# Output projection split further, stores on another queue, earlier first segments and first expert weights, in a two-block transformer kernel

## The chip, the cores and the metric

One core of one Trainium2 chip runs the whole program as one launch. The metric is the device time of a launch in microseconds (us); lower is better. The kernel before takes 3806.11 us, the median of three runs (3799.67 to 3806.13).

## The reference

1024 tokens of width 1024 in fp32 pass through two blocks.

- First block, two layers. `x = x + gate_a * (mixed @ w_out)`, where `mixed` (1024 wide) holds gated linear attention in its first 512 columns and softmax attention of 4 heads (causal, 128-query blocks) in the last 512; then a squared-ReLU MLP of width 4096. Shifts, scales and gates come from `silu(c) @ w_ada`.
- Second block, one layer. `z = rms_norm(h) @ w_in` feeds three mixers: a spatial gating unit (384 wide), a gated linear recurrence (384) and a state-space model with a GELU and a sigmoid gate (256). Each is normalised and `h = h + concat(...) @ w_out_2`. Then a router picks one of 4 groups and 2 of its 4 experts for each token (16 experts, each `(silu(x @ w_gate) * (x @ w_up)) @ w_down` of width 512), and a final norm.

## The kernel before, in words

Every engine has its own hand-written program; steps wait for each other by named semaphores (`S_.out_pe.at("turn", l, t, half)` is "TensorE has done this turn"). Tokens go in 8 tiles (`NT`) of 128, widths in 8 chunks (`KC`) of 128. A product of two fp32 operands takes either one whole fp32 matmul per chunk (two instruction records in the trace) or, split, three matmuls in the rounded type float32r: high x high, high x low, low x high (`split_mm`).

**Attention** (`sp_attention`, L1225 to L1254; `act_att_out`, L1383) has 32 steps, 4 heads of 8 query tiles in the order 7, 0, 6, 1, 5, 2, 4, 3. ScalarE writes each 128x128 result into one of two buffers, SyncE stores it to the scratch array `mixed` (64 KB), and ScalarE takes a buffer again only when its store of two steps ago has landed. All transfers of SyncE are on one queue. In between SyncE issues the loads of `w_ada` pieces (1 MB each, 16 in layer 0 and 4 in layer 1), the next head's queries, `w_out` (at steps 10 and 13, 2 MB each) and `x` (16 and 19, 2 MB each). `before_output` has SyncE, and the ScalarE step that rounds `w_out`, wait until the last two stores have landed.

**Output projection** (`pe_output`, `pe_residual`, L1473) goes tile by tile: turn 8 blocks of `mixed` (`pe_turn_mixed`), 8 chunks of matmul into two banks (the two halves of the width), turn the previous tile's normed rows. Tile 0 is whole fp32; in tiles 1 to 7 chunks 4 to 7 are whole and come first in each half, chunks 0 to 3 are split. The high part of `w_out` lies in the rows that tiles 6 and 7 of the next stage's input take later (`high_place`), the low part overwrites `w_out` itself (`dve_out_low`). VectorE does, per tile, two gated additions for each half (L1570, L1572), the low part of the turned `mixed` (`dve_mixed_low`, L1587), and the norm. The ring of `mixed` has one place: its next load is issued when the turn is done.

**End of the mixers in block two.** VectorE: gating product, scaling of `w_out_2` chunks 3 to 6, the four sums of the state-space output (L2787), two products of 3072 elements (`dve_driven`, L2478 and L2480), three scans, the last product and the last two chunks of `yT` (`dve_ssm_done`). ScalarE scales the other chunks of `w_out_2` (`act_route_weights`, L2873) after all four sigmoids. `before_route` makes every engine wait for all of it; then `pe_route` starts: per tile the norms, 16 whole matmuls in 6 segments (half 0 and half 1, each with chunks 0 to 2, 3 to 5, 6 and 7), turns and router logits.

**Experts.** 24 steps (`STEPS`), each with two blocks of 64 rows (sides 0 and 1) and each side with its own expert's weights, 2 MB each for gate, up and down, in two halves. The expert of a block is known only after the placement (`dve_placement`), so GpSimd loads weights and rows with indirect transfers; an index out of bounds skips the load when the block has the same expert as the one before. In the first step nothing is skipped. GpSimd's order is: rows of step 0, gate, up, rows of step 1, down, gate of step 1.

Of the kernel before, what the change touches and what calls it, by code (L numbers as in the profile page):

```python
# [1406 lines left out]
def output_views(k):  # L1407
# [9 lines left out]
    V.mT_hi, V.mT_lo = (k.rounded(shaped(k.weights[:, 3, n:n + SPLIT * P], (SPLIT, P))) for n in (0, KC * P))  # L1417
# [29 lines left out]

def pe_turn_mixed(k, l, t):
    S_, E, V = k.S, k.pe, k.outs
    E.wait_ge(S_.mixed_in.at(l, t))  # L1450
    for half in range(2):
        if t > 0:
            E.wait_ge(S_.out_act.at("mT", l, t - 1, half))
        if t > 1 and half == 0:
            E.wait_ge(S_.out_dve.at("mT", l, t - 1))
# [3 lines left out]
def pe_first_residual(k, l):  # L1459
# [5 lines left out]
    i.then_inc(*S_.out_pe.up("whole", l))  # L1465
# [43 lines left out]
def act_mixed_turned(k, l, t):  # L1509
    S_, E, V = k.S, k.act, k.outs  # L1510
    for half in range(2):
# [3 lines left out]
        place = V.mT_hi if half == 0 and t > 0 else V.mT[:, 4 * half:4 * half + 4, :]  # L1515
        k.nc.scalar.activation(flat(place), k.ps[half], ACT.Copy).then_inc(*S_.out_act.up("mT", l, t, half))  # L1516
# [2163 lines left out]
```

## Time and profile before

| | |
|---|---|
| Median of three runs | 3806.11 us |
| The profiled execution | 3802.61 us, of which the span is 3801.3 us |
| TensorE busy | 3602.4 us, 95% of the span |
| VectorE, ScalarE, GpSimd busy | 47%, 27%, 18% |
| Chain that ended last | TensorE 82%, VectorE 7%, DMA 4%, ScalarE 2%, GpSimd 2% |

The span is the profiled part of one execution on the chip. The chain is followed back from the last instruction, at each step to what released it. In the timeline a number in brackets is the engine's idle time before the instruction and what ended it.

### The profile page before, as it was taken

The numbers are of one execution on the slowest core, as the hardware profiler recorded it, in microseconds if no ns is written. First come the engines' busy times: TensorE is split into PE (matmuls) and PEld (weight loads), VectorE is DVE, ScalarE is ACT, GpSimd is POOL, SyncE is SP. The second block draws the span as 40 slices with busy tenths as digits, with TensorE's granted clock in tenths as the row PEclk, the third lists the DMA queues.
The fourth block names the chain that finished last, engine by engine and source line by source line (L and its number), as shares of the span: only waits on it lengthen the run. The fifth ranks groups of instructions, "written<-read, shape, count | busy, mean of one in ns | idle before, by whom it ended". The sixth has DMA issues, their size and how long they took to land.

```text
span 3801.3 us, 42410 instructions
## 1 busy us (share of the span) xinstructions
PE 3602.4 (95%) x17043; PEld 2377.4 (63%) x17043; DVE 1780.8 (47%) x3353; ACT 1035.7 (27%) x1872; POOL 693.1 (18%) x688
## 2 busy tenths in 40 slices
PE   5999899999999999998999999999999896999994
PEld 4666556777778776665567888888764553333331
DVE  5666764455555546666444334444446632000003
ACT  2444223322222224443323222222230411111111
POOL 1122001111111102211011111111010002555555
PEclk9999899999999999999999999999999997999997
DMA  6000550222222240002411111111400304887524
GB/s 218 30 29 28 181 193 28 69 79 83 78 80 90 70 163 26 26 20 87 165 34 45 45 45 56 45 45 45 136 3 0 101 28 168 319 301 259 201 82 149
DMA packets 226788, 365.55 MB, mean 96 GB/s; under 512 B 54712, under 2 KB 156946, under 8 KB 214304
## 3 DMA queue, kind: packets, MB, share of 16 engines
q1 hardware_dynamic: 176080, 240.20, 18.9%
q0 software_dynamic: 47232, 121.75, 9.0%
q8 instruction: 134, 2.20, 0.2%
q10 hardware_dynamic: 3280, 0.89, 0.1%
q14 instruction: 62, 0.51, 0.0%
HBM read 519.99 MB, written 44.04 MB: 148 GB/s over the span
## 4 chain that ended last, share of the span: by engine, by line
PE 82%; DVE 7%; DMA 4%; ACT 2%; POOL 2%; issue 2%; SPq 1%; DVEq 0%; POOLq 0%; ACTq 0%
PE psum L225 63%; PE psum L3354 13%; PE psum L233 4%; DVE arena L475 3%; DMA arena<-in_w_ada 2%; DMA tmp_mixed<-arena 1%; DVE arena L1042 0%; POOL stat L268 0%; DVE arena L416 0%; POOL stat L270 0%; POOL arena L3487 0%; PE psum L2769 0%; DMA arena<-tmp_hn,row_i 0%; DMA arena<-in_x 0%; SPq L392 0%
## 5 line engine op out<-in xcount | busy, mean ns | idle before, releaser
L225 PE MATMUL psum<-arena_r,arena_r 128*128 128x512 f32 x4096 | 1298.5, 397 | 1.0 <-POOL weight_ring_r L1838 1.0
L225 PEld LDWEIGHTS psum<-arena_r,arena_r 128*128 128x128 f32 x4096 | 768.2, 188 | 188.3 <-issue 1.9
L225 PE MATMUL psum<-arena 128*128 128x128 f32 (+9 forms) x4020 | 827.5, 382 | 11.3 <-DVE arena L1121 3.8
L225 PEld LDWEIGHTS psum<-arena 128*128 128x128 f32 (+1 forms) x4020 | 506.8, 193 | 288.7 <-issue 193.8
L225 PE MATMUL psum<-arena_r,weight_ring_r 128*128 128x512 f32 x1360 | 492.5, 399 | 0.0
L1881 DVE TENSOR_TENSOR arena<-arena,psum 128x512 f32<-128x512 f32 x512 | 335.2, 683 | 171.2 <-PE psum L225 171.1
L225 PE MATMUL psum<-weight_ring_r,arena_r 128*128 128x512 f32 x1024 | 408.7, 399 | 0.0
L1838 POOL TENSOR_TENSOR weight_ring_r<-weight_ring,arena_r 128x1024 fp32r<-128x1024 f32 x64 | 154.9, 2422 | 1126.9 <-ACT arena_r L1788 1126.9
L3354 PE MATMUL psum<-arena 128*64 128x512 f32 x1536 | 341.5, 597 | 6.4 <-DMA arena<-in_expert_w_gate,be_i 5.6
L1872 DVE TENSOR_TENSOR arena_r<-arena,arena_r 128x512 fp32r<-128x512 f32 x128 | 88.6, 692 | 462.7 <-ACT arena_r L1826 462.7
L225 PEld LDWEIGHTS psum<-arena_r,weight_ring_r 128*128 128x128 f32 x1360 | 255.7, 188 | 71.8 <-issue 13.4
L233 PEld LDWEIGHTS psum<-const,arena 128*128 128x128 f32 (+1 forms) x1439 | 171.8, 155 | 152.3 <-issue 87.3
L225 PE MATMUL psum<-weight_ring,arena 128*128 128x128 f32 (+2 forms) x1024 | 262.9, 408 | 2.5 <-DVE arena L1164 1.6
L268 POOL TENSOR_SCALAR stat<-stat 128x1 f32<-128x1 f32 (+1 forms) x120 | 43.9, 366 | 1196.6 <-ACT arena L1531 457.1
L233 PE MATMUL psum<-const,arena 128*128 128x128 f32 (+1 forms) x1439 | 214.3, 290 | 46.4 <-ACT arena L1374 16.0
L225 PE MATMUL psum<-arena,weight_ring 128*128 128x512 f32 x544 | 243.4, 600 | 7.1 <-ACT weight_ring L1516 7.1
L1802 ACT ACTIVATE arena_r<-weight_ring 128x2048 fp32r<-128x2048 f32 x32 | 61.4, 1917 | 680.5 <-DVE weight_ring L1853 680.5
L3354 PEld LDWEIGHTS psum<-arena 128*64 128x64 f32 x1536 | 108.9, 138 | 216.4 <-issue 212.7
L3445 DVE TENSOR_TENSOR arena<-arena,psum 128x512 f32<-128x512 f32 x24 | 16.5, 689 | 446.7 <-issue 287.1
L225 PEld LDWEIGHTS psum<-weight_ring_r,arena_r 128*128 128x128 f32 x1024 | 192.3, 188 | 41.8
L225 PEld LDWEIGHTS psum<-weight_ring,arena 128*128 128x128 f32 x1024 | 150.6, 197 | 85.6 <-issue 85.6
L225 PEld LDWEIGHTS psum<-arena,weight_ring 128*128 128x128 f32 x544 | 102.4, 192 | 125.1 <-issue 114.4
(380 smaller groups left out, 3372.7 us busy)
## 6 DMA issues: line engine op xcount, KB each, us to landing
weight_ring<-in_w_mlp_up SPq DMA_DIRECT2D x32, 1024.0 KB, 5.9
weight_ring<-in_w_mlp_down SPq DMA_DIRECT2D x32, 1024.0 KB, 5.0
arena<-in_w_ada SPq DMA_DIRECT2D x24, 1024.0 KB, 7.3
arena<-in_w_ada SPq DMA_DIRECT2D x40, 512.0 KB
arena<-in_w_in SPq DMA_DIRECT2D x6, 2048.0 KB, 18.6
tmp_ys<-arena SPq DMA_DIRECT2D x24, 512.0 KB
arena<-in_w_out SPq DMA_DIRECT2D x4, 2048.0 KB, 9.5
arena<-tmp_mixed SPq DMA_DIRECT2D x16, 512.0 KB, 3.3
```

Of the source, the lines that this page charges most:

```text
L225: i = self.nc.tensor.matmul(out, lhs, rhs, start=start and n == 0, stop=stop and n == len(pairs) - 1)
L233: i = self.nc.tensor.transpose(out, in_, self.ident(in_.shape[0]))
L268: k.nc.gpsimd.tensor_scalar(out, total, 1.0 / width, EPS, ALU.mult, ALU.add).then_inc(*G.up())
L475: ins = k.nc.vector.scalar_tensor_tensor(acc, V.w[:, c, :], k.cond[:, c:c + 1], acc if c else V.bias, ALU.mult, ALU.add)
L1802: k.nc.scalar.activation(down_high(k, n), V.down_w[down_slot(n)], ACT.Copy).then_inc(*S_.ff_act.up("down_hi", l, n))
L1838: k.nc.gpsimd.tensor_tensor(V.up_lo[up_slot(n)][here], w[here], V.up_hi[here].bitcast(F32), ALU.subtract).then_inc(*S_.ff_pool.up("up_lo", ...
L1872: v.tensor_tensor(V.u_lo[b][:, blk, cols], V.u[b][:, blk, cols], V.u_hi[b][:, blk, cols].bitcast(F32), ALU.subtract).then_inc(*out.up("u_l ...
L1881: v.tensor_tensor(xs, xs, ff_bank(k, down_use(m) + j), ALU.add).then_inc(*out.up("down", l, m, t, half))
L3354: i = k.nc.tensor.matmul(bank[at(c, BLOCK), :], left[:, b, at(c, BLOCK)], w[c][:, b, at(a, 512)], start=b == 0, stop=b == n - 1)
L3445: v.tensor_tensor(V.su, V.sg[s % 2], k.ps[2], ALU.mult).then_inc(*S_.ex_dve.up("su", s))
```

## The change

Six edits: (1) the attention's stores go from SyncE to GpSimd's queue; (2) in the output projection chunks 4 to 7 are split as well in tiles 2 to 5, their high part in the rows of tiles 4 and 5, and their half of `w_out` (2 MB) is loaded again for tiles 6 and 7; tiles 2 to 7 begin with split chunks 0 to 3, tile 1 has both whole halves first; (3) the first of `dve_driven`'s two products moves ahead of the state-space sums; (4) ScalarE scales chunks 0 to 2 between the sigmoids, and TensorE does the first segments of both halves of tile 0 before it waits for the rest; (5) SyncE loads expert 0's weights of side 0 ahead (gate during the route, up and down at its end), gate and down change places in memory, and GpSimd's first step takes side 1 first and skips side 0 where the first block is expert 0's; (6) the rows of step 1 are gathered before the up weights.

```diff
         E.wait_ge(S_.att_act.at("out", l, n))
-        nc.sync.dma_start(d["mixed"][at(qt), 512 + h * MV:512 + (h + 1) * MV], V.out[b]).then_inc(*(S_.att_out0 if b == 0 else S_.att_out1).dma(l, n))
...
 def pool_attention(k, l):
     before_attention(k, k.pool, l)
     pool_ada_zero(k, k.ada_att[l], l)
+    for n in range(ATT):
+        h, qt, _ = att_step(n)
+        b = n % 2
+        k.pool.wait_ge(k.S.att_act.at("out", l, n))
+        k.nc.gpsimd.dma_start(k.d["mixed"][at(qt), 512 + h * MV:512 + (h + 1) * MV], k.att.out[b]).then_inc(*(k.S.att_out0 if b == 0 else k.S.att_out1).dma(l, n))
...
-    return (V.h_lo if c < 2 else V.h_hi)[:, at(c % 2, 4), (NT - 2) * P:]
+    first = (NT - 2 if c < SPLIT else NT - 4) * P
+    return (V.h_lo if c % 4 < 2 else V.h_hi)[:, at(c % 2, 4), first:first + 2 * P]
...
+def all_split(t):
+
+    return 2 <= t < NT - 2
...
+        if t == NT - 2:
+            E.wait_ge(S_.out_pe.at("out", l, NT - 3, 1))
+            nc.sync.dma_start(V.w[:, SPLIT:], d["w_out"][l].rearrange("(k p) n -> p k n", p=P)[:, SPLIT:]).then_inc(*S_.w_again.dma(l))
...
+def pe_out_split(k, l, t, half, chunks, start):
+    S_, E, V = k.S, k.pe, k.outs
+    if start:
+        E.wait_ge(S_.out_dve.at("gated", l, t - 1, half))
+    E.wait_ge(S_.out_dve.at("w_lo", l, chunks[-1]), S_.out_dve.at("mT", l, t, chunks[-1] // 4))
+    parts = at(half, 2)
+    return k.split_mm(by_parts(k.ps[2 + half]), [(V.mT_hi[:, c, :], V.mT_lo[:, c, :], high_place(k, c)[:, parts], by_parts(V.w_lo[:, c, :])[:, parts])
+                                                 for c in chunks], start=start, stop=not start)
...
 def pe_residual(k, l, t):
     S_, E, V = k.S, k.pe, k.outs
     E.wait_ge(S_.out_act.at("mT", l, t, 1))
-    for half in range(2):
-        E.wait_ge(S_.out_dve.at("gated", l, t - 1, half))
-        k.mm(k.ps[2 + half], [(V.mT[:, c, :], V.w[:, c, at(half, 512)]) for c in range(SPLIT, KC)], stop=False)
-        E.wait_ge(S_.out_dve.at("w_lo", l), S_.out_dve.at("mT", l, t))
-        parts = at(half, 2)
-        i = k.split_mm(by_parts(k.ps[2 + half]), [(V.mT_hi[:, c, :], V.mT_lo[:, c, :], high_place(k, c)[:, parts], by_parts(V.w_lo[:, c, :])[:, parts])
-                                                  for c in range(SPLIT)], start=False)
-        i.then_inc(*S_.out_pe.up("out", l, t, half))
+    first, rest = range(SPLIT), range(SPLIT, KC)
+    if all_split(t):
+        for half in range(2):
+            pe_out_split(k, l, t, half, first, True)
+            pe_out_split(k, l, t, half, rest, False).then_inc(*S_.out_pe.up("out", l, t, half))
+    elif t == 1:
+        for half in range(2):
+            i = pe_out_whole(k, l, t, half, True)
+        i.then_inc(*S_.out_pe.up("whole", l, 1))
+        for half in range(2):
+            pe_out_split(k, l, t, half, first, False).then_inc(*S_.out_pe.up("out", l, t, half))
+    else:
+        for half in range(2):
+            pe_out_split(k, l, t, half, first, True)
+        for half in range(2):
+            pe_out_whole(k, l, t, half, False).then_inc(*S_.out_pe.up("out", l, t, half))
...
-    for c in range(SPLIT):
+    for c in range(KC):
         k.nc.scalar.activation(high_place(k, c), by_parts(V.w[:, c, :]), ACT.Copy).then_inc(*S_.out_act.up("w_hi", l, c))
...
+def dve_out_low(k, l, part):
     S_, E, V = k.S, k.dve, k.outs
-    E.wait_ge(S_.out_pe.at("whole", l))
-    for c in range(SPLIT):
+    E.wait_ge(S_.out_pe.at("whole", l, part))
+    for c in range(part * SPLIT, (part + 1) * SPLIT):
         E.wait_ge(S_.out_act.at("w_hi", l, c))
-        i = k.nc.vector.tensor_tensor(by_parts(V.w_lo[:, c, :]), by_parts(V.w[:, c, :]), high_place(k, c).bitcast(F32), ALU.subtract)
-    i.then_inc(*S_.out_dve.up("w_lo", l))
+        k.nc.vector.tensor_tensor(by_parts(V.w_lo[:, c, :]), by_parts(V.w[:, c, :]), high_place(k, c).bitcast(F32), ALU.subtract).then_inc(*S_.out_dve.up("w_lo", l, c))
...
+    for half in range(2 if all_split(t) else 1):
+        here = slice(4 * half, 4 * half + 4)
+        E.wait_ge(S_.out_act.at("mT", l, t, half))
+        k.nc.vector.tensor_tensor(flat(V.mT_lo[:, here]), k.ps[half], flat(V.mT_hi[:, here]).bitcast(F32), ALU.subtract).then_inc(*S_.out_dve.up("mT", l, t, half))
...
     for t in range(NT - 2):
+        if t == 0:
+            dve_out_low(k, l, 1)
         dve_residual(k, l, t + 1)
...
+def dve_driven_half(k):
+    S_, E, V = k.S, k.dve, k.rec
+    E.wait_ge(S_.rec_act.at("h"), S_.rec_dve.at("ix"))
+    k.nc.vector.tensor_tensor(V.i, V.i, V.h, ALU.mult).then_inc(*S_.rec_dve.up("half driven"))
+
...
 def dve_driven(k):
     S_, E, V = k.S, k.dve, k.rec
-    v = k.nc.vector
-    E.wait_ge(S_.rec_act.at("h"), S_.rec_dve.at("ix"))
-    v.tensor_tensor(V.i, V.i, V.h, ALU.mult).then_inc(*E.up())
-    E.wait_ge(S_.rec_act.at("th"), E.last)
-    v.tensor_tensor(V.i, V.i, V.th, ALU.mult).then_inc(*S_.rec_dve.up("driven"))
+    E.wait_ge(S_.rec_act.at("th"), S_.rec_dve.at("half driven"))
+    k.nc.vector.tensor_tensor(V.i, V.i, V.th, ALU.mult).then_inc(*S_.rec_dve.up("driven"))
...
         for half in range(2):
             E.wait_ge(S_.ssm_pe.at("glu", c, half))
             k.nc.scalar.activation(flat(V.gs[:, c, 4 * half:4 * half + 4]), k.ps[2 * c + half], ACT.Sigmoid, bias=k.cols[:, 50 + c:51 + c]).then_inc(*S_.ssm_act.up("glu", c, half))
+        act_route_weights(k, (S_.w_out_b, S_.w_out_c)[c], ((0, 1, 2), (7,))[c])
...
+def segment(t, j):
+
+    return ((0, 0), (1, 0), (0, 1), (0, 2), (1, 1), (1, 2))[j] if t == 0 else (j // 3, j % 3)
...
 def sp_route(k):
     nc, S_, E, V = k.nc, k.S, k.sp, k.rt
+    before_route(k, E)
     for t in range(NT):
+        if t == 1:
+            sp_first_expert(k, "gate")
         E.wait_ge(S_.rt_dve.at("hn", t))
         nc.sync.dma_start(k.d["hn"][at(t), :], V.hn).then_inc(*S_.hn_out.dma(t))
+    E.wait_ge(S_.rt_pe.at("seg", 6 * NT - 1))
+    sp_first_expert(k, "up")
+    sp_first_expert(k, "down")
...
 def pe_rt_residual(k, t):
     S_, E, V = k.S, k.pe, k.rt
     for j in range(6):
-        half, (lo, hi), u = j // 3, SEGMENTS[j % 3], 6 * t + j
+        half, part = segment(t, j)
+        (lo, hi), u = SEGMENTS[part], 6 * t + j
         if u >= 4:
             E.wait_ge(S_.rt_dve.at("seg", u - 4))
-        E.wait_ge(S_.rt_dve.at("w"), S_.rt_act.at("w", 2 if hi < KC else 7))
+        if u < 4:
+            E.wait_ge(S_.ssm_act.at("glu", u // 2, u % 2))
+        if part == 0:
+            E.wait_ge(S_.rt_act.at("w", 2))
+        else:
+            if u == 2:
+                pe_rt_norms(k, 0)
+            E.wait_ge(S_.rt_dve.at("w"), S_.ssm_dve.at("done"), S_.rec_dve.at("y"))
+        if part == 2:
+            E.wait_ge(S_.rt_act.at("w", 7))
         k.mm(k.ps[u % 4], [(k.yT[:, c, at(t)], V.w[c][:, at(half, 512)]) for c in range(lo, hi)]).then_inc(*S_.rt_pe.up("seg", u))
...
-    v.memset(V.same[:, 0:1], 0.0)
+    v.tensor_scalar(V.same[:, 0:1], V.be[:, 0:1], 0.0, None, ALU.is_equal)
...
-    V.w = {"gate": [k.arena[:, c * n:(c + 1) * n] for c in range(2)], "up": [ring[:, c * n:(c + 1) * n] for c in range(2)],
-           "down": [k.arena[:, (2 + c) * n:(3 + c) * n] for c in range(2)]}
+    V.w = {"gate": [k.arena[:, (2 + c) * n:(3 + c) * n] for c in range(2)], "up": [ring[:, c * n:(c + 1) * n] for c in range(2)],
+           "down": [k.arena[:, c * n:(c + 1) * n] for c in range(2)]}
...
+def sp_first_expert(k, what):
+    k.nc.sync.dma_start(k.ex.w[what][0], k.d[f"expert_w_{what}_2"][0][0].rearrange("(p k) n -> p (k n)", p=P)).then_inc(*first_arrived(k, what).dma())
...
+def sides(s):
+
+    return (1, 0) if s == 0 else (0, 1)
...
     if s > 0:
         E.wait_ge(S_.ex_pe.at(what, s - 1, h))
+    else:
+        E.wait_ge(first_arrived(k, what).at())
     rows = k.d[f"expert_w_{what}_2"][0].rearrange("e (p h k) n -> (e p h) (k n)", p=P, h=2)
     n = KC * D_EXP // 2
-    for c in range(2):
+    for c in sides(s):
         b = c * STEPS + s
         nc.gpsimd.indirect_dma_start(out=V.w[what][c][:, at(h, n)], out_offset=None, in_=rows, in_offset=bass.IndirectOffsetOnAxis(ap=k.place.be_i[:, h, b:b + 1], axis=0),
...
     E.wait_ge(S_.place_dve.at("be"))
     pool_load(k, "gate", 0, 0)
     pool_load(k, "gate", 0, 1)
+    pool_gather(k, 1)
     pool_load(k, "up", 0, 0)
     pool_load(k, "up", 0, 1)
-    pool_gather(k, 1)
     pool_load(k, "down", 0, 0)
...
-    E.wait_ge(arrived(k, what, h).at(s, 1))
+    E.wait_ge(arrived(k, what, h).at(s, sides(s)[1]))
...
-    act_route_weights(k)
...
     dve_route_weights(k)
+    dve_driven_half(k)
     dve_ssm_out(k)
...
```

## Rows read from the trace of the kernel before

**Rows 1.** The chain of waits, layer 0's attention: start, duration, what.
```profile
448.13 3.45 PE psum L225 x15
...
497.64 9.52 DMA tmp_mixed<-arena
```

**Rows 2.** The windows view: stretch, length, busy time of each engine, clock, DMA share, GB/s.
```profile
478.58:511.71 33.13, 31.37 (x173) 20.83 (x173) 26.29 (x60) 10.36 (x28) 0.00 (x0) 0.96 0.93 327
1829.38:1858.28 28.90, 28.16 (x159) 17.89 (x158) 14.19 (x41) 10.31 (x28) 0.00 (x0) 1.00 0.58 196
```

**Rows 3.** The timeline of ScalarE, then TensorE, where a store's landing is waited for.
```profile
507.24 0.37 ACT L1383 ACTIVATE arena<-psum,stat 128x128 f32<-128x128 f32 x1 [5.12 <-DMA tmp_mixed<-arena]
...
507.66 1.05 PE L225 MATMUL psum<-const,arena 128*128 128x1 f32 x8 [1.76 <-ACT arena L1383]
```

**Rows 4.** Groups of VectorE in layer 1's attention (1774 to 1886), by form.
```profile
L1356 DVE COPY arena<-psum 128x512 f32<-128x512 f32 x19 | 12.9, 677 | 2.3 <-PE psum L233 2.3
```

**Rows 5.** The chain of waits, layer 0's output projection.
```profile
543.99 14.02 PE psum L225 x32
...
604.83 12.59 PE psum L225 x40
617.42 1.75 PE psum L233 x16
...
661.29 5.59 PE psum L225 x24
```

**Rows 6.** The timeline of VectorE in the output projection.
```profile
551.21 4.63 DVE L1580 TENSOR_TENSOR arena_r<-arena,arena_r 128x1024 fp32r<-128x1024 f32 x4 [10.83 <-PE psum L225]
...
603.12 0.69 DVE L1570 TENSOR_TENSOR arena<-psum,gate 128x512 f32<-128x512 f32 x1 [4.80 <-PE psum L225]
...
604.46 0.68 DVE L1587 TENSOR_TENSOR weight_ring_r<-psum,weight_ring_r 128x512 fp32r<-128x512 f32 x1
```

**Rows 7.** DMA issues, 2955 to 2966: size, microseconds to landing.
```profile
weight_ring<-in_w_out SPq DMA_DIRECT2D x1, 2048.0 KB, 7.9
```

**Rows 8.** The chain of waits, end of layer 1's attention.
```profile
1883.54 3.77 DMA arena<-tmp_mixed
1889.72 16.45 PE psum L225 x32
```

**Rows 9.** The timeline of all engines before and in the route.
```profile
2982.60 2.77 ACT L2448 ACTIVATE arena<-arena 128x3072 f32<-128x3072 f32 x1
...
2987.46 0.75 DVE L2787 SCALAR_TENSOR_TENSOR arena<-arena,small,psum 128x512 f32<-128x512 f32 x1 [4.42 <-PE psum L2777]
...
2993.37 3.35 DVE L2478 TENSOR_TENSOR arena<-arena 128x3072 f32<-128x3072 f32 x1
...
3002.35 4.25 ACT L2873 ACTIVATE weight_ring<-weight_ring,small 128x1024 f32<-128x1024 f32 x4
...
3014.98 2.27 PE L225 MATMUL psum<-const,arena 128*128 128x1 f32 x10 [13.25 <-ACT arena L2946]
...
3032.88 1.17 PE L225 MATMUL psum<-const,arena 128*128 128x1 f32 x10
```

**Rows 10.** The timeline of all engines at the experts' first step.
```profile
3188.21 0.99 POOL L3306 DMA_INDIRECT arena<-in_expert_w_gate,be_i  x1 [0.30 <-issue]
...
3191.33 0.60 ACT L3405 ACTIVATE arena<-psum 128x512 f32<-128x512 f32 x1 [0.26 <-PE psum L233]
...
3196.90 9.59 PE L3354 MATMUL psum<-arena 128*64 128x512 f32 x32 [5.60 <-DMA arena<-in_expert_w_gate,be_i]
```

**Rows 11.** The chain of waits there.
```profile
3197.29 15.67 DMA arena<-tmp_hn,row_i
...
3214.97 12.48 PE psum L3354 x48
...
3228.13 10.45 PE psum L3354 x48
```

**Rows 12.** DMA queues, 3184 to 3232: packets, MB, share of 16 engines.
```profile
q0 software_dynamic: 3383, 14.74, 78.8%
```

More of the change, by code:

```diff
@@ L1233, in sp_attention @@
     for n in range(ATT):
-        h, qt, _ = att_step(n)
-        b = n % 2
+        h = n // NT
         if n % 2 == 1 and n // 2 + 4 < 2 * len(place.pieces):
@@ L1416, in output_views @@
     V.w_lo = k.rounded(V.w)
-    V.mT_hi, V.mT_lo = (k.rounded(shaped(k.weights[:, 3, n:n + SPLIT * P], (SPLIT, P))) for n in (0, KC * P))
+    V.mT_hi, V.mT_lo = (k.rounded(shaped(k.weights[:, 3, n:n + KC * P], (KC, P))) for n in (0, KC * P))
 SPLIT = 4
@@ L1454, in pe_turn_mixed @@
         if t > 1 and half == 0:
-            E.wait_ge(S_.out_dve.at("mT", l, t - 1))
+            E.wait_ge(S_.out_dve.at("mT", l, t - 1, 0))
+        if all_split(t - 1) and half == 1:
+            E.wait_ge(S_.out_dve.at("mT", l, t - 1, 1))
         k.turn4(k.ps[half], V.mixed, half).then_inc(*S_.out_pe.up("turn", l, t, half))
@@ L1464, in pe_first_residual @@
         i = k.mm(k.ps[2 + half], [(V.mT[:, c, :], V.w[:, c, at(half, 512)]) for c in range(SPLIT)], stop=False)
-    i.then_inc(*S_.out_pe.up("whole", l))
+    i.then_inc(*S_.out_pe.up("whole", l, 0))
     for half in range(2):
@@ L1468, in pe_first_residual, with pe_out_whole @@
         i.then_inc(*S_.out_pe.up("out", l, 0, half))
+def pe_out_whole(k, l, t, half, start):
+    S_, E, V = k.S, k.pe, k.outs
+    if start:
+        E.wait_ge(S_.out_dve.at("gated", l, t - 1, half))
+    elif t == NT - 2:
+        E.wait_ge(S_.w_again.at(l))
+    return k.mm(k.ps[2 + half], [(V.mT[:, c, :], V.w[:, c, at(half, 512)]) for c in range(SPLIT, KC)], start=start, stop=not start)
+def pe_out_split(k, l, t, half, chunks, start):
+    S_, E, V = k.S, k.pe, k.outs
+    if start:
+        E.wait_ge(S_.out_dve.at("gated", l, t - 1, half))
+    E.wait_ge(S_.out_dve.at("w_lo", l, chunks[-1]), S_.out_dve.at("mT", l, t, chunks[-1] // 4))
+    parts = at(half, 2)
+    return k.split_mm(by_parts(k.ps[2 + half]), [(V.mT_hi[:, c, :], V.mT_lo[:, c, :], high_place(k, c)[:, parts], by_parts(V.w_lo[:, c, :])[:, parts])
+                                                 for c in chunks], start=start, stop=not start)
 def pe_residual(k, l, t):
@@ L1514, in act_mixed_turned @@
             E.wait_ge(S_.out_pe.at("out", l, t - 1, 1))
-        place = V.mT_hi if half == 0 and t > 0 else V.mT[:, 4 * half:4 * half + 4, :]
-        k.nc.scalar.activation(flat(place), k.ps[half], ACT.Copy).then_inc(*S_.out_act.up("mT", l, t, half))
+        place = V.mT_hi if half == 0 and t > 0 or all_split(t) else V.mT
+        k.nc.scalar.activation(flat(place[:, 4 * half:4 * half + 4, :]), k.ps[half], ACT.Copy).then_inc(*S_.out_act.up("mT", l, t, half))
 def act_out_high(k, l):
@@ L1618, in dve_output @@
     k.dve.wait_ge(k.S.x_all_in.at(l, 4))
-    dve_out_low(k, l)
+    dve_out_low(k, l, 0)
     dve_residual(k, l, 0)
@@ L2921, in pe_route @@
     S_, E, V = k.S, k.pe, k.rt
-    before_route(k, E)
-    pe_rt_norms(k, 0)
     pe_rt_residual(k, 0)
@@ L3024, in dve_rt_residual @@
     for j in range(6):
-        half, seg, u = j // 3, j % 3, 6 * t + j
+        (half, seg), u = segment(t, j), 6 * t + j
         xs, bank = V.x[:, t, at(half, 512)], k.ps[u % 4]
@@ L3294, in pool_gather, with first_arrived @@
                                  in_offset=bass.IndirectOffsetOnAxis(ap=k.place.row_i[:, s:s + 1], axis=0)).then_inc(*rows_arrived(k, s).dma(s))
+def first_arrived(k, what):
+    return {"gate": k.S.eg_first, "up": k.S.eu_first, "down": k.S.ed_first}[what]
+def sp_first_expert(k, what):
+    k.nc.sync.dma_start(k.ex.w[what][0], k.d[f"expert_w_{what}_2"][0][0].rearrange("(p k) n -> p (k n)", p=P)).then_inc(*first_arrived(k, what).dma())
+def sides(s):
+    return (1, 0) if s == 0 else (0, 1)
 def pool_load(k, what, s, h):
```

12 lines of the change are left out of this document (4 added, 8 removed).

## The prediction

> **What bounds the kernel now.** I read the page first: TensorE is busy in nearly every one of the 40 slices, and the chain that ended last is mostly TensorE. So time goes in two ways only: fewer or cheaper matmuls where TensorE never waits, or less of the few gaps in which it does. The chain cut to stretches shows which is which. In the output projection it is TensorE alone, 12.59 us of matmuls and 1.75 us of turns for each tile [rows 5]: a full engine, with gaps only around tiles 0 and 1. In layer 0's attention a small store takes 9.52 us and the chain runs through it [rows 1, 3]. Before the route the chain is VectorE's, and TensorE stood 13.25 us idle [rows 9]. At the experts' start it is transfers: TensorE waits 5.60 us for gate weights, and then the second gather needs 15.67 us to land [rows 10, 11]. The 24 expert steps after that are TensorE's and are untouched.
>
> **Edit 1, stores on GpSimd's queue.** What holds the store in layer 0 is the queue that it shares with loads of 1 and 2 MB: the head from 478.58 takes 33.13 us at a DMA share of 0.93, the same head in layer 1, with 4 `w_ada` loads instead of 16, takes 28.90 us [rows 2]. Not all of the 4.23 us is the store: the head before it (448.13 to 478.58, 30.45 us [rows 1, 2]) has VectorE's `w_ada` sums too and no such wait. I take 33.13 - 30.45 = 2.7 us, with 0 and 4.2 as ends. In GpSimd's queue are 32 issues for each layer; the trace has no plain GpSimd transfer. The nearest row is an indirect one, 0.99 us to issue [rows 10], against a lap of 28.90 / 4 = 7.2 us for two stores, and GpSimd is idle there [rows 2]. The last store lands perhaps 1 to 2 us later, which delays ScalarE's rounding of `w_out` and SyncE's loads; tile 0's 14.02 us of whole matmuls [rows 5] hide that. SyncE keeps its waits for `out`, so its loads come no sooner. One cost could speak against the edit: a GpSimd transfer that is held up by VectorE. VectorE's copies in attention take 677 ns for 512 elements [rows 4], 1.3 ns an element, read from PSUM. The Trainium skill, "SBUF — State Buffer", section "SBUF: two separate sides", says that VectorE's two-port modes, as in fp32 copies from SBUF to SBUF, lock GpSimd out so that it can't write descriptors. By that rule copies at this rate from PSUM shouldn't lock it, so the sum stays; were it otherwise it would be the third rival.
>
> **Edit 2, chunks 4 to 7 split.** A split chunk is three matmuls. 24 of them take 5.59 us [rows 5], 0.233 each; a tile with all chunks split has 48, 11.18 us, against 12.59 us: 1.41 us less. Four tiles: 5.64 us for each layer. Three things take from it.
> First, VectorE's low part of `mixed` was needed only after the whole chunks; now tiles 2 to 7 begin with split ones. VectorE ends it at 604.46 + 0.68 = 605.14, and TensorE began that tile at 604.83 [rows 5, 6]. With the semaphore that is 0.4 us of stall in each of tiles 3 to 7, 2.0 us. In the all-split tiles VectorE has another 0.68 us, but the second half's part is wanted 2.8 us later: hidden.
> Second, tile 2: VectorE's second `dve_out_low` (4.63 us [rows 6]) can start only when tile 1's whole chunks are done, 5.59 us before that tile's end; then come the four additions, 0.69 us each, and the low part. It ends about -5.6 + 0.15 + 4.6 + 2.7 + 0.7 = 2.6 us after the tile, and TensorE wants it 1.75 us after: 0.8 us. ScalarE's four more roundings fall before it is next needed.
> Third, the reload. 2 MB landed in 7.9 us with little beside it [rows 7]. TensorE wants it after turns, stall and 24 matmuls: 1.75 + 0.4 + 5.59 = 7.7 us after tile 5's end, at which it is issued: 0.3 us. The next `mixed` tile queues behind it on SyncE's queue and is wanted 6.8 us of whole matmuls later: hidden.
> Together 5.64 - 2.0 - 0.8 - 0.3 = 2.5 us for each layer, 5.1 us for both. Ends: +11.3 if no stall shows, -4.8 if each of six tiles stalls by 1.0 us and the reload by 2.
>
> **Edits 3 and 4, the hand-over to the route.** `h` is ready at 2982.60 + 2.77 = 2985.37, and VectorE stands 4.42 us idle before 2987.46 [rows 9]. The first product (3.35 us) fits from 2985.4 to 2988.8; the first sum is 1.3 us late, the last one at 2992.7 isn't. So the whole chain after it is 3.35 us shorter, and the norms start at about 3011.6 instead of 3014.98. SyncE's load of `x` waits on the same chain and moves with it.
> The two first segments are 6 of tile 0's 16 whole matmuls, 16 of which take 14.02 us [rows 5]: 5.26 us. ScalarE's scaling of three chunks is done by 3005.5 even if it starts no sooner than now (3002.35, 1.06 us each [rows 9]), and TensorE has the segments done by 3010.8, inside its gap. What is left is the 17.9 us from 3014.98 to 3032.88 [rows 9] less 5.26 us: tile 0 ends at 3011.6 + 12.6 = 3024.2, 8.6 us sooner. In this the slow clock stays as it is: norms took 2.27 us where the next ones took 1.17, and layer 1's 16 whole matmuls after a wait of 3.77 us took 16.45 us instead of 14.02 [rows 5, 8]. The gap that remains is about 1 to 4 us; if the clock stays high the gain is 11.0 us, if the product's move is lost elsewhere 5.3. The later tiles run as before. The 2 MB of gate weights on SyncE's queue go between two `hn` stores that 16 whole matmuls, 14 us, keep apart; at 7.9 us they are hidden.
>
> **Edits 5 and 6, the first expert step.** Now the chain is gate (3196.90), second gather (lands 3212.96), up weights' matmuls from 3214.97 [rows 10, 11]. 14.74 MB move on GpSimd's queue in 48 us, nearly all in the first 32 [rows 12]; of them 6 MB are side 0 of step 0 and are skipped if the first block is expert 0's. The gate's first half is then 1 MB instead of 2 and issued one place sooner, before 3188.21 [rows 10]: it lands before or near 3192.5, when the turned rows are ready too (3191.33 + 0.60 = 3191.93). Gate: 3192.5 + 9.59 = 3202.1. The second gather, now ahead of 4 issues and behind 2 MB, has landed by then. Its turns take 1.0, so the up matmuls start at 3203.1, 11.9 us sooner. They took 12.48 us for 48 where the steady 48 take 10.45 [rows 11]: with no gap ahead of them up to 2.0 us more come back. The rest of the loads comes at the same spacing as before while TensorE is 12 us ahead, so some of this may be lost again: I take 12.5 us, ends 7.5 (gate no sooner, the gather alone) and 14. The preloads of up and down, 4 MB, have the placement's 20 us to land. The new `tensor_scalar` instead of a memset is some 0.1 us.
>
> **Sum.** 2.7 + 5.1 + 8.6 + 12.5 = 28.9 us. The profiled execution took 3802.61 us around a span of 3801.3, so it would take 3773.7. The median of the runs is 3.5 us above it: 3806.11 - 28.9 = **3777 us**.
>
> **Rivals.**
> The start of the experts gives less: the first block isn't expert 0's and nothing is skipped, so the preload does nothing (the change doesn't do what it says), or the loads behind bind. Only the gather's place counts, 7.5 us: 3782. For it: 2 MB of gate took until 3196.9. Against: 128 assignments for each expert on average, so an empty expert 0 is unlikely.
> The output projection costs instead of giving: at the bound of -4.8 us the total is 19 us, 3787. For it: VectorE and TensorE hand over at each tile's end. Against: only 0.4 us is seen missing.
> The other side: stores from GpSimd are slow. ScalarE was ready for its buffer at 502.1, 4.5 us after the store's issue at 497.64, and TensorE lost 1.76 us of a landing of 9.52 [rows 1, 3]; so a landing up to some 7.8 us costs nothing. If each pair's store took 9.52 us, 16 pairs in 2 layers would lose 1.76 each, 56 us in place of the gain: 3806 + 56 - 26 = 3836. It decides from a landing of 7.8 us, and turns the whole slower from 8.6 (26 / 32 above it). Against: 64 KB alone, on a queue of its own, with 0.99 us of issue.
>
> **How the numbers follow.** The sum as worked out 0.72, less at the experts 0.12, output at a loss 0.10, slow stores 0.04, something unseen 0.02. Adding the ends, the gain lies between 8 and 40.5 us; both ends need every term at its worst or best, so I cut to 3764 to 3791. A measurement of this kernel tells 0.2%, 7.6 us, from nothing: faster 0.93, within 0.2% 0.03, slower 0.04.
>
> **What would show each step.** After: (1) no wait of ScalarE's L1383 for a store, layer 0's third head near 30.4 us, stores landing in under 4.5 us; (2) 11.2 us for tiles 2 to 5 of both layers, a gap of 0.3 to 0.5 before each tile from 2 on, nearly 1 before tile 2, and before tile 6's whole chunks under 1; (3, 4) the norms of tile 0 near 3.4 us sooner than the rest of the program's shift, six matmuls ahead of them, tile 0 done 8 to 11 us sooner; (5, 6) gate weights no longer the wait, gathers landing in about 5 us, the first up matmuls 12 to 14 us sooner after placement. Wrong would be: a tile period that stays at 14.3, a clock that drops at the new gaps, an expert step 1 that waits for its gate weights, or a store of 8 us.

## The result, and the profile after

The changed kernel takes 3775.69 us, the median of four runs (3775.22 to 3780.64), against 3806.12 us for the one before in the same session (3799.67 to 3808.91): a ratio of 0.9925 [0.9908, 0.9943], 0.75% less. Forecast were 3777 us. Its profiled execution took 3776.03 us, 26.6 us less than that of the kernel before. Numbers in steps below are from the two profiled executions; at each joint I subtract the start of the same piece of work after from its start before, so the growth of this offset from joint to joint is what a stretch gave. "The logits" stands for the start of the router's last logit matmuls (x16, 3.6 us).

The head of the page: the span, then each engine's busy time, share and instructions.

```profile
span 3774.7 us, 42602 instructions
...
PE 3589.2 (95%) x17107; PEld 2385.5 (63%) x17107; DVE 1794.1 (48%) x3369; ACT 1042.6 (28%) x1880; POOL 729.1 (19%) x752
```

TensorE is 13 us less busy, so half of the gain is time in which it used to stand.

| Stretch | Forecast gain, us | Measured |
|---|---|---|
| Layer 0's attention (edit 1) | 2.7 | 3.7 |
| Output projection, layers 0 and 1 (edit 2) | 2.5 and 2.5 | -0.66 and -0.53 |
| To the end of the scans (edit 3) | 3.35 | 3.46 |
| The row above and on to tile 2 of the route (edits 3, 4) | 8.6 | 9.87 |
| Placement to step 1 (edits 5, 6) | 12.5 | 12.46 |
| All else | 0 | 1.72 |
| Sum (the 3.46 us are in the 9.87), span | 28.9 | 26.6 |

"All else" is small pieces of both signs (start-up +1.2, MLPs -1.7, layer 1's attention and tile 0 +1.9, the rest of the route +1.7, the tail -1.4); I take no cause for them from one execution each.

**Attention.** The chain of waits in layer 0 (start, duration, what) answers to [rows 1]: the store is gone from it.

```profile
477.39 3.45 PE psum L225 x15
...
507.85 3.45 PE psum L225 x15
```

The windows view (stretch, length, busy time of PE, PEld, DVE, ACT, POOL, clock, DMA share, GB/s) answers to [rows 2] with its first line (the second is for the output projection below):

```profile
477.39:507.85 30.46, 29.95 (x175) 19.69 (x174) 25.80 (x59) 10.24 (x28) 4.32 (x8) 1.00 0.93 342
556.79:565.64 8.85, 8.85 (x17) 3.92 (x18) 0.85 (x2) 0.00 (x0) 0.00 (x0) 0.81 0.03 11
```

The third head takes 30.46 us where it took 33.13, at the same DMA share of 0.93. The waits view of ScalarE between 412 and 545 us had its L1383 wait four times, 10.8 us in all, for a store's landing; after, one wait of 1.1 us is left, that of the rounding before the output projection. All 64 stores of attention, in the view of their line (issue time minimum, median, maximum in ns; then the landings):

```profile
L1262 POOL DMA_DIRECT2D tmp_mixed<-arena x64: 540/540/807, 421.9 to 1881.8; - x64
...
DMA to landing us min/median/max: 1.9/3.5/6.2
```

**Output projection.** The chain of layer 0 answers to [rows 5], with its last two lines from layer 1:

```profile
539.07 14.02 PE psum L225 x32
556.79 8.85 PE psum L225 x16
...
573.69 11.44 PE psum L225 x48
587.32 11.45 PE psum L225 x48
...
614.59 11.45 PE psum L225 x48
626.05 8.03 DMA arena<-in_w_out
634.12 7.15 PE psum L225 x16
643.46 12.71 PE psum L225 x40
657.04 5.59 PE psum L225 x24
...
1886.08 15.64 PE psum L225 x32
1905.43 8.85 PE psum L225 x16
```

An all-split tile has 48 matmuls in 11.44 us and a period of 13.63 (573.69 to 587.32), where a tile had 12.59 and 14.34. Tiles 6 and 7 take 13.05 (634.12 + 7.15 - 628.22, the timeline's start of tile 6) and 12.71 us. But tile 1 lost: its 16 whole records, now all in front, take 8.85 us at a mean granted clock of 0.81 (second line of the windows above), where the same 16 take 7.15 us in tile 6.

**Before the route.** The timeline (start, duration, instruction, in brackets the idle time before it and what ended that) answers to [rows 9]:

```profile
2989.43 3.35 DVE L2529 TENSOR_TENSOR arena<-arena 128x3072 f32<-128x3072 f32 x1
...
3000.04 5.39 PE L225 MATMUL psum<-weight_ring,arena 128*128 128x512 f32 x12 [0.55 <-ACT weight_ring L2922]
3007.61 1.25 PE L225 MATMUL psum<-const,arena 128*128 128x1 f32 x10 [2.18 <-ACT arena L3014]
3008.71 10.53 PE L225 MATMUL psum<-weight_ring,arena 128*128 128x512 f32 x20
...
3019.08 1.17 PE L225 MATMUL psum<-const,arena 128*128 128x1 f32 x10
```

One product is left after the sums; six matmuls (12 records) stand in the old gap; ahead of the norms 2.18 us of idleness are left of 13.25, and the norms take 1.25 us where they took 2.27. The 20 records behind them are slow: 10.53 us, where the later tiles' 32 take 13.98, which is 8.74 for 20. The windows view of TensorE's clock shows why:

```profile
3009.00:3012.37 3.37, 3.37 (x5) 1.34 (x4) 1.41 (x4) 0.63 (x1) 0.70 (x1) 0.50 0.64 21
```

The chain at the experts answers to [rows 11]:

```profile
3148.55 3.61 PE psum L225 x16
3172.67 5.95 DMA arena<-in_expert_w_gate,be_i
3178.75 9.20 PE psum L3438 x32
3189.04 10.45 PE psum L3438 x48
3200.17 10.45 PE psum L3438 x48
```

The gather's 15.67 us are off the chain, and the first 48 up records take 10.45 us, not 12.48. GpSimd's queue moved 119.66 MB in this execution and 125.95 MB in no_preload below: the 6 MB of side 0 were indeed skipped.

### The profile page after: what moved, and what is told of

Its sections match the earlier page's. It is cut to its first block, busy times and chain, and to the rows that moved or that the text cites. A ratio compares the mean times of both kernels' runs of the same rounds, so it can differ in the third digit from the quotient of the medians.

```text
span 3774.7 us, 42602 instructions
## 1 busy us (share of the span) xinstructions
PE 3589.2 (95%) x17107; PEld 2385.5 (63%) x17107; DVE 1794.1 (48%) x3369; ACT 1042.6 (28%) x1880; POOL 729.1 (19%) x752
## 3 DMA queue, kind: packets, MB, share of 16 engines
q0 software_dynamic: 49280, 119.66, 9.0%
## 4 chain that ended last, share of the span: by engine, by line
PE 82%; DVE 8%; DMA 4%; POOL 2%; ACT 2%; issue 2%; SPq 0%; DVEq 0%; POOLq 0%; ACTq 0%
PE psum L225 64%; PE psum L3438 13%; PE psum L233 4%; DVE arena L475 3%; DMA arena<-in_w_ada 2%; DVE arena L416 1%; POOL arena L3571 1%; POOL stat L268 1%; DMA weight_ring<-in_w_ada 0%; DVE arena L1042 0%; POOL stat L270 0%; PE psum L2818 0%; DVE stat L1338 0%; DVE arena L1099 0%; DVE arena L1927 0%
## 5 line engine op out<-in xcount | busy, mean ns | idle before, releaser
L225 PE MATMUL psum<-arena_r,weight_ring_r 128*128 128x512 f32 x1552 | 525.6, 392 | 6.0 <-DVE weight_ring_r L1631 6.0
L225 PEld LDWEIGHTS psum<-arena_r,weight_ring_r 128*128 128x128 f32 x1552 | 290.8, 188 | 77.9 <-ACT weight_ring_r L1559 5.9
L225 PE MATMUL psum<-arena,weight_ring 128*128 128x512 f32 x416 | 186.5, 607 | 7.0 <-ACT weight_ring L1559 6.9
L3438 PE MATMUL psum<-weight_ring,arena 128*64 128x512 f32 x768 | 170.0, 595 | 0.0
```

The lines of the kernel that those rows point to most:

```text
L225: i = self.nc.tensor.matmul(out, lhs, rhs, start=start and n == 0, stop=stop and n == len(pairs) - 1)
L3438: i = k.nc.tensor.matmul(bank[at(c, BLOCK), :], left[:, b, at(c, BLOCK)], w[c][:, b, at(a, 512)], start=b == 0, stop=b == n - 1)
```

## The experiments

Runs named together in a heading shared a chip and its runs of the kernel before. What was disputed: whether the output projection's missing 3 us a layer come from VectorE's late low part (as forecast) or from TensorE's slow stretch in tile 1, and what starts that one; and for each other edit, whether the part named pays.

### out_old, low_first, low_first_alt, t1_whole_first

The kernel before took 3808.51 us there (3804.74 to 3811.78, 7 runs).

**out_old**: the changed kernel with all functions of the output projection as they were before.

```diff
-    if all_split(t):
...
+    for half in range(2):
+        E.wait_ge(S_.out_dve.at("gated", l, t - 1, half))
+        k.mm(k.ps[2 + half], [(V.mT[:, c, :], V.w[:, c, at(half, 512)]) for c in range(SPLIT, KC)], stop=False)
...
```

> The changed kernel with the output projection as it was before the change (edit 2 undone, all else kept). My theory: the output projection gave nothing and cost about 0.6 us in each layer, since a slow clock in tile 1, 0.7 us before tile 2, 0.45 us before each later tile and a split rate of 0.238 instead of 0.233 us a matmul take back the 5.6 us of the cheaper chunks. Then layer 0's stretch from tile 1's first matmul to the last tile's turn is 99.6 us as before instead of 100.2, and the whole is 0 to 2 us faster than the changed kernel: 3774 to 3776. Rival: the edit did give its 5 us in the whole time, and something else (an extra wait elsewhere) hides it in the trace: then this takes 3780 or more.

Measured: 3779.88 us (3778.14 to 3781.95), 0.9925 [0.9909, 0.9942], where the changed kernel had the same ratio in its own session. My forecast of 3774 to 3776 us was missed, and 3780 was the mark of the rival, by which the edit does give its 5 us. But changed_again below, on the same chip, has 3775.90 us and 0.9917 [0.9903, 0.9931], and the intervals overlap: in the whole time edit 2 gives nothing that can be told from none. The stretches tell more. From tile 1 to the last turn layer 0 takes 98.69 us, like before (98.71), and layer 1 takes 100.37: tile 1 of layer 1 has the slow stretch even with the old order (14.41 us where layer 0's has 12.72).

**low_first**: VectorE makes the low part of the next tile between the two halves' additions.

```diff
-        dve_residual(k, l, t + 1)
-        dve_mixed_low(k, l, t + 2)
+        dve_gate(k, l, t + 1, 0)
+        dve_add(k, l, t + 1, 0)
+        dve_gate(k, l, t + 1, 1)
+        dve_mixed_low(k, l, t + 2, (0,))
+        dve_add(k, l, t + 1, 1)
+        if all_split(t + 2):
+            dve_mixed_low(k, l, t + 2, (1,))
```

> The changed kernel; VectorE takes the low part of the next tile's turned rows before the last addition of the tile. My theory: the gap before each of tiles 2 to 7 is VectorE's hand-over, so it falls from 0.45 us to 0 in five tiles and from 0.7 to about 0 in tile 2: tile period in tiles 2 to 5 13.2 instead of 13.63 us, some 2.9 us less for each layer, 5 to 6 us in all, about 3770. Rival: the gap is a cost of TensorE's own in going from turns to split matmuls: the period stays at 13.6 and the time at 3776.

Measured: 3774.23 us (3771.63 to 3778.28), 0.9908 [0.9891, 0.9924]. The timeline of TensorE:

```profile
574.47 11.44 PE L225 MATMUL psum<-arena_r,weight_ring_r 128*128 128x512 f32 x48 [0.19 <-DVE weight_ring_r L1640]
587.86 11.43 PE L225 MATMUL psum<-arena_r,weight_ring_r 128*128 128x512 f32 x48 [0.19 <-DVE weight_ring_r L1640]
```

The period falls from 13.63 to 13.39 us. The pause doesn't go, as I had expected, it shrinks from 0.44 us (0.46 in the timeline) to 0.19: that rest is the way from the turn over ScalarE's rounding to VectorE's subtraction. VectorE itself waits 0.38 us for ScalarE there, so another order of VectorE would not shorten it.

**low_first_alt**: as low_first, and in tile 1 whole and split chunks alternate by half as they did before; VectorE's second `dve_out_low` is cut in two around the hand-over.

```diff
         for half in range(2):
             i = pe_out_whole(k, l, t, half, True)
-        i.then_inc(*S_.out_pe.up("whole", l, 1))
-        for half in range(2):
+            if half == 1:
+                i.then_inc(*S_.out_pe.up("whole", l, 1))
             pe_out_split(k, l, t, half, first, False).then_inc(*S_.out_pe.up("out", l, t, half))
...
-            dve_out_low(k, l, 1)
+            dve_out_low(k, l, 1, range(2))
...
+            dve_out_low(k, l, 1, range(2, 4))
+            dve_mixed_low(k, l, t + 2, (1,))
+            dve_add(k, l, t + 1, 0)
```

> As low_first, and tile 1 again takes whole and split chunks in turn for each half, with VectorE's second rounding of the weights divided around the hand-over (two chunks before it, two after). My theory: the slow clock in tile 1 comes with 16 whole matmul records in a row after the gap; with 8 in a row tile 1's chunks take 12.7 us as before the change instead of 15.0, so 1.7 to 2.3 us less for each layer beyond low_first: about 3766. Rival: the low clock comes from the gap alone, or from what lies before it: tile 1 stays at 15.0 us and this is no faster than low_first.

Measured: 3772.83 us (3769.81 to 3775.06), 0.9907 [0.9891, 0.9924], not apart from low_first. Its chain:

```profile
558.26 12.72 PE psum L225 x40
572.93 11.50 PE psum L225 x48
...
1904.42 14.41 PE psum L225 x40
```

Tile 1 of layer 0 is at full clock, tile 1 of layer 1 isn't, with the same order of matmuls in both; in low_first it was slow in both (14.42 us).

**t1_whole_first**: the kernel before, with tile 1's two whole halves first; one execution.

```diff
+    if t == 1:
+        for half in range(2):
+            E.wait_ge(S_.out_dve.at("gated", l, t - 1, half))
+            k.mm(k.ps[2 + half], [(V.mT[:, c, :], V.w[:, c, at(half, 512)]) for c in range(SPLIT, KC)], stop=False)
     for half in range(2):
-        E.wait_ge(S_.out_dve.at("gated", l, t - 1, half))
+        if t > 1:
...
```

> The kernel before with one edit: in tile 1 both halves' whole chunks come first, then both halves' split ones. My theory (the order brings the slow clock): the 16 whole records take about 8.8 us and tile 1 about 14.5 us where the kernel before has 12.7, in both layers. Rival (something that the changed kernel does ahead of tile 1 brings it, such as the stores or ScalarE's four more roundings): tile 1 stays at 12.7 us.

Measured: 3806.02 us. Its chain:

```profile
562.34 12.72 PE psum L225 x40
...
1910.85 12.74 PE psum L225 x40
```

Sixteen whole records in a row, and no slow stretch in tile 1. My first theory, that this order of matmuls brings it, falls by this run, and by out_old and low_first_alt, which have the old order and the slow stretch in layer 1.

### sync_store, gather_late, no_preload, segments_old

One execution each; the kernel before took 3803.48 us there.

**sync_store**: the changed kernel with the stores on SyncE's queue again.

```diff
+        nc.sync.dma_start(d["mixed"][at(qt), 512 + h * MV:512 + (h + 1) * MV], V.out[b]).then_inc(*(S_.att_out0 if b == 0 else S_.att_out1).dma(l, n))
...
-        k.nc.gpsimd.dma_start(k.d["mixed"][at(qt), 512 + h * MV:512 + (h + 1) * MV], k.att.out[b]).then_inc(*(k.S.att_out0 if b == 0 else k.S.att_out1).dma(l, n))
```

> The changed kernel with edit 1 undone: attention's stores on SyncE's queue again. My theory: in layer 0 the head that starts near 477 takes 33.1 us instead of 30.46, with a wait of ScalarE for a store's landing near 5 us, and the attention ends 3 to 4 us later; layer 1's attention changes by under 0.5 us. Rival: the gain of that head came from another edit or from the run, and it stays at 30.5. On the slow clock in tile 1 of the output projection, which the last runs showed with and without the order of edit 2: if it hangs on edit 1's timing at the attention's end, tile 1 of both layers is back at full clock here; if it comes by chance or by edit 2, it is not.

Measured: 3784.97 us. The chain in layer 0's attention:

```profile
486.69 10.63 DMA tmp_mixed<-arena
497.79 9.53 DMA tmp_mixed<-arena
```

ScalarE waits 12.2 us in four waits for stores, and from the second head (457.92) to tile 0 (546.63) it takes 88.71 us; gather_late, with the stores on GpSimd's queue, takes 81.74 (458.19 to 539.93), and the changed kernel 81.71. The two long landings come back with the queue. That is 7.0 us, more than the 3 to 4 expected: the third head takes 34.53 us (477.95 to 512.48), 4.1 more than in the changed kernel, and the other 2.9 lie behind it, where TensorE is also at 1.2 GHz for some 3.4 us from 542.3. Tile 1 is at full clock in both layers here (7.15 us for its 16 whole records).

**gather_late**: the rows of step 1 after the up weights again.

```diff
-    pool_gather(k, 1)
     pool_load(k, "up", 0, 0)
     pool_load(k, "up", 0, 1)
+    pool_gather(k, 1)
```

> The changed kernel with edit 6 undone: the rows of step 1 gathered after the up weights again. My theory: with the preload only 4 MB lie ahead of that gather instead of 8, so it lands about 5 us later than in the changed kernel but before the gate matmuls end or within 1 us of it: the first up matmuls come 0 to 1.5 us later. Rival: the gather's place is what gave most of the 12.5 us; then the up matmuls start 5 us or more later.

Measured: 3777.28 us. From the logits (3150.48) to the third block of expert matmuls (3202.84) it takes 52.36 us; the changed kernel takes 51.62 (3148.55 to 3200.17). The gather lands 6.84 us after its issue and TensorE waits 1.37 us for it. With the preload in place edit 6 is worth 0.74 us.

**no_preload**: no `sp_first_expert`, nothing skipped in step 0, the gather still early.

```diff
-            sp_first_expert(k, "gate")
...
-    sp_first_expert(k, "up")
-    sp_first_expert(k, "down")
...
-    v.tensor_scalar(V.same[:, 0:1], V.be[:, 0:1], 0.0, None, ALU.is_equal)
+    v.memset(V.same[:, 0:1], 0.0)
...
-    return (1, 0) if s == 0 else (0, 1)
+    return (0, 1)
```

> The changed kernel with edit 5 undone (no weights of expert 0 loaded ahead, nothing skipped in the first step, side 0 first), the early gather kept. My theory: the gate weights come 4 to 5 us later again and the up weights 4 MB later, so the steady steps start 5 to 8 us later than in the changed kernel, leaving 5 to 7 us of the 12.5. Rival: the early gather alone gives it all: within 1 us of the changed kernel.

Measured: 3789.15 us. Its chain:

```profile
3145.67 3.62 PE psum L225 x16
3186.55 18.82 DMA arena<-in_expert_w_gate,be_i
3205.51 6.21 PE psum L3431 x16
3212.39 10.45 PE psum L3431 x48
```

From the logits to that last line it takes 66.72 us, 15.1 more than the changed kernel and 2.6 more than the kernel before (3164.05 to 3228.13, 64.08). The gather is on time, and now step 1's gate weights land last: 18.82 us after their issue, with TensorE idle for 6.79 us. I had expected 5 to 7 of the 12.5 us to stay; nothing stays. So the early gather alone is worth less than nothing here, and what pays is the 6 MB taken off the queue. (This kernel also keeps the changed places of gate and down in memory; their part was not told apart.)

**segments_old**: tile 0's segments in the old order after `before_route` and the norms, scaling after all four sigmoids; the early product stays.

```diff
-    return ((0, 0), (1, 0), (0, 1), (0, 2), (1, 1), (1, 2))[j] if t == 0 else (j // 3, j % 3)
+    return (j // 3, j % 3)
...
+    before_route(k, k.pe)
+    pe_rt_norms(k, 0)
     pe_rt_residual(k, 0)
```

> The changed kernel with edit 4 undone (segments of tile 0 in the old order after the common wait, and the weights scaled after all sigmoids), edit 3 kept. My theory: the six whole matmuls come back onto the path and TensorE's gap is 10 us again, so tile 2 of the route starts 5.3 us later by the matmuls and 1 to 2 us more by the slower clock after the longer gap, 6.3 to 7.3 us in all. Rival: the gap's length doesn't matter to the clock: 5.3 us.

Measured: 3781.35 us. Start of the scans to tile 2 of the route: 49.68 us (2990.71 to 3040.39), against 42.14 in the changed kernel (2992.82 to 3034.96): edit 4 is worth 7.5 us by this pair, and 6.4 against the kernel before (3000.21 to 3048.76, 48.55 us), whose 32 records of tile 0 took 1.1 us less than those of segments_old (15.94 against 17.05). I had expected 6.3 to 7.3.

### no_gap, all_three, changed_again

The kernel before took 3807.99 us there (3803.29 to 3809.50, 9 runs). By then the slow stretch of tile 1 was seen only together with two things: a gap of 2.6 to 2.85 us ahead of tile 1, and stores on GpSimd's queue. The gap is ScalarE's: it norms tile 0 before it copies the second half of the turned `mixed`, for which TensorE waits.

**no_gap**:

```diff
-    act_normed(k, l, 0)
     act_mixed_turned(k, l, 1)
+    act_normed(k, l, 0)
```

> The changed kernel with one edit: ScalarE copies the turned rows of tile 1 before it squares tile 0's rows, so TensorE no longer stands 2.6 to 2.9 us between tile 0 and tile 1 of the output projection. My theory: the slow clock in tile 1 (16 whole records in 8.8 us instead of 7.1), seen in layer 1 of every kernel with the stores on GpSimd's queue and in none with them on SyncE's, needs that gap: with about 1 us of gap tile 1 runs at full clock in both layers, and each layer is 1.5 to 2 us shorter by the gap and up to 1.7 by the clock: 3769 to 3773. Rival: the slow clock follows from the wait before tile 0 and comes some 20 us after it whatever lies between: then it stays in layer 1, perhaps at another tile, and only the gap's 1.5 to 2 us are gained.

Measured: 3773.93 us (3770.98 to 3774.77), 0.9912 [0.9897, 0.9927]. The timeline of TensorE at tile 1, first in the changed kernel:

```profile
556.79 8.83 PE L225 MATMUL psum<-arena,weight_ring 128*128 128x512 f32 x16 [2.57 <-ACT weight_ring L1559]
```

then in no_gap:

```profile
555.04 7.13 PE L225 MATMUL psum<-arena,weight_ring 128*128 128x512 f32 x16 [0.80 <-ACT weight_ring L1559]
```

The gap falls to 0.80 us and the 16 records are at full clock, in layer 1 as well (7.13 from 1902.95). But in layer 1 tile 0 now takes 16.74 us instead of 15.64: the slow time is still there, in one piece ahead of and in tile 0 (windows under "Open" below). From tile 0's start to the last turn: 113.34 and 116.12 us.

**all_three**: low_first_alt with the same swap.

> low_first_alt and no_gap together, the version that the runs so far point to. My theory: 1.4 us (VectorE's order and tile 1's) and 1.5 to 2 us (gap) for each layer plus the clock's 1.7 in layer 1, in all 7 to 9 us under the changed kernel: 3767 to 3769, a ratio of 0.990 to the kernel before on one chip. Rival: the two share the same wait (tile 1's start) and add to only 4 us.

Measured: 3770.89 us (3766.50 to 3772.22), 0.9900 [0.9885, 0.9915], the fastest here. Its chain:

```profile
556.77 12.72 PE psum L225 x40
571.43 11.50 PE psum L225 x48
...
1885.57 15.39 PE psum L225 x32
1902.63 12.72 PE psum L225 x40
```

From tile 0's start to the last turn: 111.90 and 113.34 us.

**changed_again**: the changed kernel, unaltered.

> The changed kernel once more, unaltered, on the same chip as the two above, so that they can be compared directly. Both theories: 3775 to 3780 and a ratio of 0.992 to 0.993 to the kernel before; on the slow clock in tile 1: present in layer 1, in layer 0 either way.

Measured: 3775.90 us (3771.30 to 3781.74), 0.9917 [0.9903, 0.9931]; from tile 0's start to the last turn 117.06 and 118.45 us, tile 1 slow in both layers (8.85). all_three is 5.1 us shorter in each layer, some 1.7 of them by tile 1's clock; in the medians 5.0 us in all show, and the intervals of the ratios overlap, so the order of the two is likely and no more.

## Why the prediction was right or wrong

Three of the four terms of the sum came out, the experts' to 0.04 us, the other two low by 1.0 and 1.3. The fourth, edit 2, had the wrong sign: 6.3 us less than forecast. Unplanned pieces gave 1.7 us. So the profiled execution took 3776.03 us against a forecast of 3773.7. That it came so near is in part luck, since 6.3 us too little met 4.0 us too much, and that the median is 1.3 us on the other side of 3777 is luck too: the profiled execution of before lay 3.5 us under its median, that of after 0.3 above.

**Edit 1, right, and low.** The third head fell by 2.67 us, as worked out; 1.0 us more came elsewhere in the layer. My sign for it, landings under 4.5 us, was wrong: in that head all of them took 4.9 to 6.2 us, where before they were spread from 1.6 to 9.8. What pays is that none exceeds what two steps of ScalarE cover, and that bound (7.8 us) was the one in the text. An issue costs GpSimd 0.54 us, not 0.99. The third rival falls, and sync_store confirms the cause.

**Edit 2, the step that failed: "Together 5.64 - 2.0 - 0.8 - 0.3 = 2.5 us for each layer".** The pauses were right (0.44 us against 0.4, tile 2's 0.74 against 0.8), and so was the reload: it landed in 8.03 us, and tile 6 took 0.34 us longer than tile 7 (0.2 in layer 1), against 0.3. Two other terms weren't. First, 48 matmuls in a row take 0.238 us each, not the 0.233 of the 24 that I scaled up (that row, the last of [rows 5], is the MLP's first, behind the last turn): 0.26 us in each of four tiles, and 0.12 in tiles 6 and 7 each, 1.3 us. Second, tile 1's clock: +1.70 us in each layer, which was not in the sum at all; the text named "a clock that drops at the new gaps" only as something that would make it wrong. 2.5 - 1.3 - 1.7 = -0.5, against -0.66 and -0.53 measured. The slow stretch isn't edit 2's own doing: out_old, without the edit, has it in layer 1 (14.41 us), and gather_late and segments_old, with the edit and changed only some 2400 us later or more, don't have it in layer 0. Without it the edit gives 1.04 us a layer (out_old against the changed kernel, both slow in tile 1 of layer 1: 100.37 - 99.24 = 1.13), less than the spread of the runs. The second rival (a loss there) came true in sign, at -1.2 us for both layers instead of -9.6, and by another mechanism.

**Edits 3 and 4, right.** 3.46 and then 6.41 us. Of the latter 5.24 is the six matmuls (12 records at 13.98 / 32 each) and 1.2 the clock. Tile 0, from its norms on, took 17.90 us before where the next tile takes 14.85, so 3.05 were lost at 1.2 GHz; after, it takes 11.47 where 14.85 - 5.24 = 9.61 would do, so 1.86 are lost. The clock fell again, for 3.4 us just behind the norms, though only 2.18 us of waiting were left. That lies between "stays as it is" (8.6) and "stays high" (11.0), and the forecast took the lower one.

**Edits 5 and 6, right as a sum.** Inside it the parts were off: the gate's matmuls began 2.65 us sooner against the logits, not 4.4, and the up matmuls 10.4 us sooner, not 11.9; at full pace instead of 12.48 us they gave the 2.0 us named. The lower end, "gate no sooner, the gather alone", 7.5 us, was wrong, and with it the first rival's price: no_preload shows that case at -2.6 us. I had priced the gather's place with the load of its queue left out.

**Open.** Why tile 1's first matmuls run slowly. Of the eight kernels with stores on GpSimd's queue and a gap of 2.6 us or more, all eight have it in layer 1, and none of the three with stores on SyncE's. That looks like a rule of tile 1, but the clock of the whole stretch says otherwise. Windows in layer 1 where it is 0.50, first the kernel before, then two of the changed kernel, then no_gap:

```profile
1887.84:1894.66 6.82, 6.13 (x13) 2.98 (x11) 0.00 (x0) 4.98 (x6) 0.00 (x0) 0.50 0.89 282
1885.98:1889.38 3.40, 3.30 (x4) 1.51 (x5) 0.00 (x0) 3.40 (x5) 0.00 (x0) 0.50 1.02 318
1906.46:1909.86 3.40, 3.40 (x6) 1.32 (x5) 0.00 (x0) 0.00 (x0) 0.00 (x0) 0.50 0.01 2
1883.27:1890.08 6.81, 6.12 (x11) 2.62 (x10) 0.00 (x0) 6.75 (x9) 0.00 (x0) 0.50 0.91 291
```

From the wait ahead of tile 0 to the end of tile 1, TensorE is at 1.2 GHz for 6.8 us in the kernel before, in the changed kernel and in no_gap; it only lies in one piece or in two. The second piece is tile 1's slow stretch. Of all thirteen traces only all_three has less in layer 1, 3.4 us. In layer 0 the slow piece comes in four of the eight kernels with the same gap, also in the unaltered changed kernel both times, and not in no_gap or all_three. So no_gap moved the slow time of layer 1 and did not remove it; that the gap ahead of tile 1 is needed for it isn't shown, nor what the queue does to it. no_gap's sure gain is the shorter gap.

## What to carry to other kernels

Price a denser stretch of matmuls by the time of a full-length row at its own count, and read the granted clock of the whole stretch around each wait, before and after, and not of one tile: 1.7 us for 16 records ate all that four split tiles gave, and a slow piece that is gone from one tile can be found in the one before it. A small store that something waits for belongs on a queue that big loads don't use, even if each issue costs more. Moving one transfer ahead of others on a full queue only changed which one was late; taking bytes off the queue paid.

## What the runs showed of the hardware

- The granted clock falls to 1.2 GHz near short waits too. 16 matmul records behind a wait of 2.57 us (layer 0) or 2.85 us (layer 1) took 8.85 us at a mean of 0.81 between the levels of 1.2 and 2.4 GHz, with 14 to 16 us of matmuls in a row ahead of the wait. In the route the clock was 0.50 from 3009.00 to 3012.37, 1.4 us of matmuls after a wait of 2.18 us, and 16 records from 2990.66, behind a wait of 1.96 us, took 8.83 us where the kernel before took 7.13 behind the same 1.96. The length of the wait alone does not decide: in gather_late 2.62 us ahead of tile 1 of layer 0 left the clock at 1.00.
- A plain 64 KB store takes GpSimd 0.54 us to issue (0.81 at most, 64 of them) and lands after 1.9/3.5/6.2 us (minimum, median, maximum); from SyncE it was 0.32 us and 1.5/2.2/9.8. GpSimd's is the slower one in all but the longest landing, and it is the longest that is waited for: sync_store loses 7 us in layer 0. The Trainium skill, "DMA: Bandwidth & Descriptors", section "Issuing engine by pattern", gives simple stores to SyncE as the faster way; the minimum and the median here agree, the longest landing and the kernel's time don't. In the third head SyncE's queue also carried five loads of 1 MB and two of 2 MB.
- VectorE's copies out of PSUM beside these issues never held one up beyond 0.81 us. By the rule of the Trainium skill, "SBUF — State Buffer", section "SBUF: two separate sides", weighed in the forecast, they shouldn't, and the trace agrees.
- 48 split matmuls in a row take 0.238 us each, 24 take 0.233.
